# A model step on one core: the first quad of weights in pieces of two units, and a warm-up cut in two

## The reference

```python
def even_mixer(h, w_in, conv_w, pool_w, pool_scale, w_out):
    z = h @ w_in                       # h: rmsnorm of x, 256 x 1024; w_in: 1024 x 2048
    gate_b = z[..., :A_W]
    gate_c = z[..., A_W:2 * A_W]
    val = z[..., 2 * A_W:3 * A_W]
    pool_in = z[..., 3 * A_W:]
    y_a = gate_b * causal_dwconv(gate_c * val, conv_w)
    y_b = multiscale_pool(pool_in, pool_w, pool_scale)
    return jnp.concatenate([y_a, y_b], axis=-1) @ w_out
```

## Time and profile before

| | |
|---|---|
| median of 3 runs | 908.39 us (908.06 to 908.59) |
| the profiled execution | 908.13 us |
| its span, first to last instruction | 906.4 us |
| TensorE busy | 898.8 us, 99% |
| VectorE, ScalarE, GpSimd busy | 669.0, 572.4, 244.9 us |
| read from memory, written | 161.71 MB, 3.44 MB |

### The profile page before, as it was taken

The page is one execution under the profiler, slowest core; times in us unless marked ns, Lnnn a source line. Parts: engine busy times, 40 slices in busy tenths (PEclk is TensorE's granted clock), DMA queues, the critical chain, the costliest instruction groups (busy, mean ns, idle before and its releaser), DMA issues.

```text
span 906.4 us, 18290 instructions
## 1 busy us (share of the span) xinstructions
PE 898.8 (99%) x6030; PEld 814.9 (90%) x6030; DVE 669.0 (74%) x1352; ACT 572.4 (63%) x997; POOL 244.9 (27%) x130
## 2 busy tenths in 40 slices
PE   9999999999999999999999999999999999999997
PEld 9999888888899999988888888999998888888897
DVE  7987887786656756688777866788667766686566
ACT  7456776774445556576666644667758877774453
POOL 0421544420000002044443000350104988850000
PEclk9999999999999999999999999999999999999999
DMA  8655677678534444456666654344335655576531
GB/s 300 200 170 164 210 238 241 199 237 270 171 118 140 140 132 151 161 169 212 228 188 219 229 191 142 116 164 141 117 120 182 210 190 191 192 238 208 184 97 47
DMA packets 47194, 163.51 MB, mean 180 GB/s; under 512 B 5235, under 2 KB 10099, under 8 KB 47142
## 3 DMA queue, kind: packets, MB, share of 16 engines
q1 hardware_dynamic: 42336, 158.12, 53.6%
q10 hardware_dynamic: 4805, 4.70, 1.5%
HBM read 161.71 MB, written 3.44 MB: 182 GB/s over the span
## 4 chain that ended last, share of the span: by engine, by line
PE 94%; DVE 3%; ACT 2%; issue 1%; DVEq 0%; ACTq 0%
PE psum L1528 40%; PE psum L1529 20%; PE psum L1552 7%; PE psum L1553 7%; PE psum L1554 7%; PE psum L1675 2%; PE psum L1677 1%; PE psum L1678 1%; PE psum L1788 1%; DVE wl L974 1%; PE psum L1891 1%; PE psum L1763 1%; ACT wh L577 1%; PE psum L1727 1%; PE psum L1725 1%
## 5 line engine op out<-in xcount | busy, mean ns | idle before, releaser
L577 ACT ACTIVATE wh<-raw 128x1024 fp32r<-128x1024 f32 (+2 forms) x266 | 297.1, 1119 | 113.3 <-PE psum L1529 80.6
L1528 PE MATMUL psum<-xs,wh 128*128 128x512 f32 x1056 | 367.2, 394 | 0.0
L515 POOL TENSOR_TENSOR wl<-raw,wh 128x1024 fp32r<-128x1024 f32 (+1 forms) x86 | 209.4, 2440 | 457.7 <-ACT wh L577 456.2
L1529 PE MATMUL psum<-xs,wl 128*128 128x256 f32 x1056 | 292.7, 277 | 0.0
L974 DVE TENSOR_TENSOR wl<-raw,wh 128x1024 fp32r<-128x1024 f32 (+2 forms) x180 | 241.0, 1343 | 52.1 <-ACT wh L577 51.8
L1528 PEld LDWEIGHTS psum<-xs,wh 128*128 128x128 f32 x1056 | 198.0, 188 | 45.9
L1529 PEld LDWEIGHTS psum<-xs,wl 128*128 128x128 f32 x1056 | 198.3, 188 | 0.1
L1528 PE MATMUL psum<-ys,wh 128*128 128x512 f32 x528 | 183.2, 394 | 0.0
L1529 PE MATMUL psum<-ys,wl 128*128 128x256 f32 x528 | 146.3, 277 | 0.0
L1552 PE MATMUL psum<-xs,wh 128*128 128x256 f32 x416 | 120.3, 289 | 0.0
L1528 PEld LDWEIGHTS psum<-ys,wh 128*128 128x128 f32 x528 | 99.0, 188 | 23.0
(11 more groups left out here) (239 smaller groups left out, 1232.7 us busy)
## 6 DMA issues: line engine op xcount, KB each, us to landing
raw<-in_up SPq DMA_DIRECT2D x132, 512.0 KB, 3.4
raw<-in_down SPq DMA_DIRECT2D x48, 704.0 KB, 4.4
raw<-in_qkv SPq DMA_DIRECT2D x48, 512.0 KB, 3.3
raw<-in_out SPq DMA_DIRECT2D x16, 512.0 KB, 3.3
raw<-in_even_in SPq DMA_DIRECT2D x12, 512.0 KB, 3.6
raw<-in_ple SPq DMA_DIRECT2D x8, 640.0 KB, 3.9
raw<-in_even_out SPq DMA_DIRECT2D x8, 512.0 KB, 3.6
raw<-in_even_in SPq DMA_DIRECT2D x8, 256.0 KB, 5.6
```

The costliest lines, as they stand in the source:

```text
L515: nc.gpsimd.tensor_tensor(low, raw[:, s, 0:tiles * P], high.bitcast(f32), ALU.subtract)\
L577: nc.scalar.activation(split_weights(q, s, tiles * P)[0], raw[:, s, 0:tiles * P], ACT.Copy).then_inc(hi_ready, 1)
L1528: nc.tensor.matmul(bank, wh[:, s, w], inputs(t), start=first, stop=False)
L1529: done = nc.tensor.matmul(bank[:, SEQ:2 * SEQ], wl[:, s, w], inputs(t)[:, 0, :], start=False, stop=last)
```

## The change

The 96 products of the first quad stay, and so do the bytes. What differs:

- The first quad's weights are laid out anew on the host (`pieces_first`): a slot's half now holds two tiles of two units. Slot 0 has tiles 0 to 3 of units 0 and 1 (first half: tiles 0 and 1 of both), slot 1 tiles 4 to 7 of units 0 and 1, slots 2 and 3 the same for units 2 and 3.
- TensorE takes tiles 0, 1 of all four units, then tiles 2, 3 of all four, then tiles 4 to 7 of units 0 and 1, then of unit 2, then of unit 3.
- SyncE's loads, ScalarE's roundings and scalings and VectorE's splits get a new order; the first half of slot 0 leads, ahead of the first x.
- `WARM_UP` is 4 products, then the tables' product, then 2 more.
- On ScalarE's queue `onehot` and `rel` go out ahead of the scales.
- On SyncE's queue `pool_w` goes out right behind the pieces, then the first unit of the next quad, once slot 0 is split, then the vectors and `counts`, then the other three units.

```diff
-WARM_UP = 12
+WARM_UP = (4, 2)
+PIECES = ((0, 0), (2, 0), (0, 1), (2, 1), (1, 0), (1, 1), (3, 0), (3, 1))
+PIECE_COUNT = {piece: [p for p in PIECES if p[1] == piece[1]].index(piece) + 1 for piece in PIECES}
...
+            load_half(0, 0)
             load_x(0)
-            load_half(0, 0)
+            load_half(2, 0)
+            load_half(0, 1)
+            load_x(1)
+            load_half(2, 1)
+            load_x(2)
             load_half(1, 0)
-            load_x(1)
-            load_half(2, 0)
+            load_x(3)
+            load_half(1, 1)
             load_half(3, 0)
-            load_x(2)
-            load_half(0, 1)
-            load_half(1, 1)
-            load_x(3)
-            load_half(2, 1)
             load_half(3, 1)
+            sp.dma_start(pool_w, pool_in).then_inc(pool_landed, 16)
+
+            sp.wait_ge(lo_ready[0], 1)
+            load_unit("even_in", 1, 0)
             sp.dma_start(vec[:, DC:], vectors_in[:, DC:]).then_inc(vectors_landed, 16)
-            for tile, source in ((counts, count_in), (pool_w, pool_in)):
-                sp.dma_start(tile, source).then_inc(pool_landed, 16)
+            sp.dma_start(counts, count_in).then_inc(pool_landed, 16)
...
-            act.dma_start(vec[:, 0:DC], vectors_in[:, 0:DC]).then_inc(scales_landed, 16)
             for tile, source in ((onehot, onehot_in), (rel, rel_in)):
                 act.dma_start(tile, source).then_inc(tables_landed, 16)
+            act.dma_start(vec[:, 0:DC], vectors_in[:, 0:DC]).then_inc(scales_landed, 16)
...
+            round_half(0, 0)
             act.wait_ge(scales_landed, 16)
             scale_x(0)
...
+            split_half(0, 0)
+            for n, pieces in enumerate((((2, 0), (0, 1)), ((2, 1),), ((1, 0),), ((1, 1), (3, 0), (3, 1)))):
                 for m in (2 * n, 2 * n + 1):
                     norm_low(0, m)
-
-                for unit, half in (((0, 0), (1, 0)), ((2, 0), (3, 0)), ((0, 1), (1, 1)), ((2, 1), (3, 1)))[n]:
+                for unit, half in pieces:
                     split_half(unit, half)
...
-            warm(WARM_UP, aux[:, 1, 0:P])
+            warm(WARM_UP[0], aux[:, 1, 0:P])
             tables()
+            warm(WARM_UP[1], aux[:, 1, 0:P])
+
+            def first_part(s, n):
+
+                slot, half = s // 2 * 2 + n // 2, n % 2
+                pe.wait_ge(lo_ready[slot] if half else lo_half, 1 if half else PIECE_COUNT[slot, 0])
+                for t in (2 * n, 2 * n + 1):
                     pe.wait_ge(xl_ready, t + 1)
+                    at = half * HALF_UNIT + s % 2 * 2 * P + t % 2 * P
+                    w = slice(at, at + P)
...
-            for half in range(2):
-                for n in (2 * half, 2 * half + 1):
-                    for s in range(2):
-                        first_part(s, range(2 * n, 2 * n + 2))
-                for s in range(2, RING):
-                    first_part(s, range(half * DC // 2, (half + 1) * DC // 2))
+            for n in range(2):
+                for s in range(RING):
+                    first_part(s, n)
+            for n in (2, 3):
+                for s in range(2):
+                    first_part(s, n)
+            for s in range(2, RING):
+                for n in (2, 3):
+                    first_part(s, n)
```

More of the change, by code:

```diff
@@ L462, in load_half, with load_quad @@
                 sp.dma_start(raw[:, s, part], streams["even_in"][s, :, part]).then_inc(raw_landed[s] if half else half_landed[s], 16)
+            load_half(0, 0)
             load_x(0)
-            load_half(0, 0)
+            load_half(2, 0)
[3 more added lines that the diff above has]
+            load_x(2)
             load_half(1, 0)
-            load_x(1)
-            load_half(2, 0)
+            load_x(3)
+            load_half(1, 1)
             load_half(3, 0)
-            load_x(2)
-            load_half(0, 1)
-            load_half(1, 1)
-            load_x(3)
-            load_half(2, 1)
             load_half(3, 1)
+            sp.dma_start(pool_w, pool_in).then_inc(pool_landed, 16)
+            sp.wait_ge(lo_ready[0], 1)
+            load_unit("even_in", 1, 0)
             sp.dma_start(vec[:, DC:], vectors_in[:, DC:]).then_inc(vectors_landed, 16)
-            for tile, source in ((counts, count_in), (pool_w, pool_in)):
-                sp.dma_start(tile, source).then_inc(pool_landed, 16)
+            sp.dma_start(counts, count_in).then_inc(pool_landed, 16)
             for name, quads, _ in PHASES:
-                def load_quad(i):
+                def load_quad(i, first=0):
                     q = i + base[name]
-                    for s in range(RING):
+                    for s in range(first, RING):
                         sp.wait_ge(lo_ready[s], q)
@@ L486, in _ @@
                 if name == "even_in":
-                    load_quad(1)
+                    load_quad(1, 1)
                     for tile, source in ((p_raw, p_in), (gate_w[:, :, :], gate_in)):
@@ L628, in round_half @@
                 nc.scalar.activation(wh[:, s, part], raw[:, s, part], ACT.Copy).then_inc(hi_ready if half else hi_half, 1)
+            round_half(0, 0)
             act.wait_ge(scales_landed, 16)
             scale_x(0)
-            round_half(0, 0)
+            round_half(2, 0)
+            round_half(0, 1)
+            scale_x(1)
+            round_half(2, 1)
+            scale_x(2)
             round_half(1, 0)
-            scale_x(1)
-            round_half(2, 0)
+            scale_x(3)
+            round_half(1, 1)
             round_half(3, 0)
[L637 to L641, removed]
             round_half(3, 1)
@@ L1042, in split_half @@
                 part = slice(half * HALF_UNIT, (half + 1) * HALF_UNIT)
-                dve.wait_ge(hi_ready if half else hi_half, s + 1)
+                dve.wait_ge(hi_ready if half else hi_half, PIECE_COUNT[s, half])
                 nc.vector.tensor_tensor(wl[:, s, part], raw[:, s, part], wh[:, s, part].bitcast(f32), ALU.subtract)\
                   .then_inc(lo_ready[s] if half else lo_half, 1)
-            for n in range(4):
+            split_half(0, 0)
+            for n, pieces in enumerate((((2, 0), (0, 1)), ((2, 1),), ((1, 0),), ((1, 1), (3, 0), (3, 1)))):
                 for m in (2 * n, 2 * n + 1):
                     norm_low(0, m)
-                for unit, half in (((0, 0), (1, 0)), ((2, 0), (3, 0)), ((0, 1), (1, 1)), ((2, 1), (3, 1)))[n]:
+                for unit, half in pieces:
                     split_half(unit, half)
@@ L1891, in warm @@
                     nc.tensor.matmul(bank, ones[:, :], ones[:, :], start=True, stop=True)
-            warm(WARM_UP, aux[:, 1, 0:P])
+            warm(WARM_UP[0], aux[:, 1, 0:P])
             tables()
-            def first_part(s, tiles):
-                pe.wait_ge(lo_ready[s] if tiles[0] >= DC // 2 else lo_half, 1 if tiles[0] >= DC // 2 else s + 1)
-                for t in tiles:
-                    pe.wait_ge(xl_ready, t + 1)
[L1901 to L1905, removed]
+            warm(WARM_UP[1], aux[:, 1, 0:P])
[3 more added lines that the diff above has]
+                for t in (2 * n, 2 * n + 1):
+                    pe.wait_ge(xl_ready, t + 1)
+                    at = half * HALF_UNIT + s % 2 * 2 * P + t % 2 * P
+                    w = slice(at, at + P)
+                    nc.tensor.matmul(slot_bank(s), wh[:, slot, w], xs[:, t, 0, :], start=t == 0, stop=False)
+                    nc.tensor.matmul(slot_bank(s), wh[:, slot, w], xs[:, t, 1, :], start=False, stop=False)
+                    last = nc.tensor.matmul(slot_bank(s), wl[:, slot, w], xs[:, t, 0, :], start=False, stop=t == DC - 1)
+                if n == 3:
                     last.then_inc(units_done, 1)
@@ L2015, in projection_units, with pieces_first @@
     return np.ascontiguousarray(np.stack(units))
+def pieces_first(units):
+    first = units[:RING].reshape(2, 2, P, 2, 2, 2 * P).transpose(0, 3, 2, 4, 1, 5).reshape(RING, P, DC * P)
+    return np.ascontiguousarray(np.concatenate([first, units[RING:]]))
 def channel_columns(v):
@@ L2046 @@
     natural = list(range(DC))
-    arrays["even_in"] = weight_units(a["ev_w_in"][0], even_order)
+    arrays["even_in"] = pieces_first(weight_units(a["ev_w_in"][0], even_order))
     by_turns = np.arange(D).reshape(2, D // 2 // P, P).transpose(1, 0, 2).reshape(-1)
```

## The result

The change makes the kernel slower by 0.24%: 910.70 us in the median of 14 runs (909.70 to 911.31) against 908.44 (908.06 to 908.93, 14 runs), 2.3 us; the ratio is 1.0024 with a 95% interval of 1.0017 to 1.0032. The forecast was 908.0 with a range up to 909.8. Besides the shift, the spread is wider: 1.6 us between the fastest and the slowest run, where it was 0.9.

The account below looks back on a forecast made before the run. TensorE, busy 99% of the span, was taken as the bound, its start set by the warm-up. Start -0.37, second-unit stall -0.1 and late loads +0.1 gave -0.4 us: 908.0 us against 908.39, range 907.1 to 909.8.

Parts of the forecast that it names:

- What bounds the kernel: TensorE, busy 99% of the span, runs without a notable gap; only its start, its clock or a new wait can move the time.
- the choice that the clock rises near 5.2: TensorE's clock goes to the full level near 5.2 us as before, despite the gap ahead of the tables' product; chance 0.45.
- The sum: Whole kernel: start -0.37, second-unit stall -0.1, starving and late loads +0.1; total -0.4 us.
- the 0.1 stall at the second unit: TensorE's loss before its second unit's first product, gone because one piece serves both units: -0.1 us.
- Rival 1: TensorE's clock rises late, at 8.7 us, as the gap restarts its count: 909.4 us; chance 0.30.
- Part 2: TensorE's tables' product waits for its input, landing at 4.7 (4.2 to 5.1); it ends at about 5.9, the later warm-ups at 6.3.
- Part 3: Scales, last in ScalarE's queue, land at 5.5 (5.1 to 6.4); first product at 6.55 against 6.92.
- Part 4: First quad's pieces feed TensorE with 0.0 to 0.8 us to spare; up to 0.3 us stall carried, 0.1 us stall gone.
- Part 5: SyncE's reordered queue and the next quad's split, done at 18.7, cost 0, or up to 0.2 us if the split slips.

Follow-up runs that it names:

- small products: Kernel before with four small products (33 partitions, 18 columns) between the sixth and seventh warm-up: 911.12 us, ratio 1.0037.
- the runs with 6 warm-ups: Changed kernel with the scales first, 6 warm-ups in one stretch and the tables' product behind the first 24 products: 910.09 us, ratio 1.0018.

## Why the prediction was wrong, point by point

**What bounds the kernel** (right). TensorE sets the end, and a microsecond lost ahead of the first quad's end is lost for good: +3.06 us there, +3.1 in the span.

**The step that failed: the choice that the clock rises near 5.2.** The sum took 4 + 2 warm-ups with a gap as no worse for the clock than 12 in a row, for want of a row with a gap. The clock rose at about 12.4. The price in the profiled execution: the tables' product and the later warm-ups at the low level, 1.89 + 1.15 where 0.96 + 0.4 stood in the sum, then 19 products from 8.42 to 12.62, 4.2 us, where 19 x 0.12 + 0.2 = 2.5 would do: 1.7 us. (The 0.2 is the first product's start, 0.32 us in the chain of before where the pitch is 0.12.) The first product came 8.42 - 6.99 = 1.43 us late; 1.43 + 1.7 less the 0.1 stall at the second unit that is gone is 3.0 of the 3.06 us. That the warm-up edit is the cause is shown from both sides: made alone in the kernel before it costs 2.8 us, and with it and the scales' place undone the changed kernel is back at 908.32.

**Rival 1** named this mechanism and was mis-sized. Its rise at 8.7 counted 4 us from the start of the tables' product at 4.7, but that product doesn't do what a warm-up does (small products above). The rise came 7 us behind the tables' product's start and 5.2 us behind its end at 7.26. Counted from that end, 4 us would have given 11.3, still 1.1 short. And the trace of before gave one execution's rise, where the profiles have it at 4.5 to 6.0 us and the runs with 10 warm-ups show the same program on both sides. A range built on it had to be wider above.

**Part 2, the landing of the tables' input** (mis-sized). 4.7 with an upper bound of 5.1; it was 5.33, 3.85 us from its issue. Being issued 0.45 us sooner brought it forward only 0.2 against the version with the scales first (5.53). Nor did it land sooner after its issue for the 128 small packets that were gone from ahead of it, on which I had counted: 3.85 us without them, 3.61 with them.

**Part 3, the scales** (mis-sized; harmless here). 5.5 with an upper end of 6.4; the landing was 7.0 and 7.6 in two profiles. The row that I held to be nearest, the third place of the same queue, gave 3.6 us; they took 5.2 and 5.8. In the changed kernel this hid behind TensorE's own front: putting them first again did not help (911.34). With unbroken warm-ups it costs some 0.4 to 0.6 us in eight runs of 11, and in the profile where it made TensorE stand 1.9 us behind the tables' product the clock was lost as well.

**Part 4, pieces and order** (right in its sum, for a start at 7). With both other edits undone the median is 0.2 us lower than before and the interval holds 1. The walk through the landings was too smooth. In one profile the second piece landed at 6.86 where 6.3 was put, and the start at 6.17 lost 0.7 us there; the second piece of x landed at 8.66 and 9.2 in two profiles, where 7.9 was put for the fifth place. In another execution a start at 6.38 met no wait at all. So from 6.55 part of the 0.4 us gain could have been lost, in some executions and not in others; no run starts there with the tables' product in front.

**Part 5, SyncE's queue and the next quad's split** (right in its price, wrong in one step). No profile has a wait for a load behind the first quad. But the split of the next quad's first unit, put at 18.7 as before, was over only at 19.48 with both edits undone, and TensorE lost 0.24 us there, close to the forecast's "from 0 to 0.2 us if the split slips". It slipped with the squares: ScalarE, which stood for the second piece of x until 8.66 and then worked without a break, ended its last rounding at 14.0 where it was 13.25, and the sum for the statistics began at 15.85 instead of 15.09. In the changed kernel TensorE is 3 us late itself and the split, over at 20.68, costs nothing.

What stays open: why the landings of the first pieces differ by 1 us and more between executions (the second piece of x by 7.9 in one profile, at 9.2 in another), and in which proportion the gap and the tables' product delay the clock in the changed kernel. Each of them alone is enough to do it, as the runs with 6 warm-ups and with the small products show; the two together were not taken apart.

## What to carry to other kernels

In this kernel the warm-up is not idle filling that can be cut to what the inputs leave over: it has to be one unbroken stretch of full-size products that reaches past the latest rise seen, not past the rise of one trace, with nothing behind a landing and no small product inside it. Price such an edit by a second level of the clock over everything up to the next possible rise, not over the stretch that was cut. Where a median doesn't move but the runs split in two groups (10 warm-ups: 908.0 and 910.0), the edit has reached an edge. And work that is moved out of the way still has its own time: the tables' product cost 0.96 us behind the first 24 products as well.

## What the runs showed of the hardware that was not expected

- Unbroken work of 4.6 us (20 warm-up records) had not raised the clock in one profile, while about 4 us had in the kernel before; over six profiles of unbroken warm-ups begun at 1.1 us the first faster record starts between 4.5 and 6.0 us.
- 1.9 us of small products (33 partitions, 18 columns) between two stretches of full ones left the clock at 1.2 GHz to 8.6 us without any gap; with 16 full warm-ups in one stretch it had risen by 6.2.
- A clock that had risen fell back to 1.2 GHz at about 8.5 us, behind 1.03 us of the small tables' product and 1.6 us of the gap that followed, in one profile and by the times in three of 11 runs.
- A 4 KB transfer of 128 small packets, third in its queue, took 5.2 to 5.8 us from issue to landing; first in its queue it took 3.3.
- The granted-clock column of the windows read 1.00 over nearly 4 us (8.4 to 12.4) in which every product ran at the low level. In the one profile in which the clock had risen and fallen again, it showed the fall (0.50 from 8.5 to 11.5).
